# The norms' inverse roots as the exponential of minus half a logarithm on ScalarE, in a two-block transformer kernel

## The reference

```python
def rmsnorm(x, w):
    y = x32 * lax.rsqrt(jnp.mean(x32 * x32, axis=-1, keepdims=True) + EPS)
    return (y * w.astype(jnp.float32)).astype(x.dtype)

u = rmsnorm(h, norm1_w[l]) * (1.0 + sc1) + sh1            # block 1, before w_in
o = rmsnorm(o, gnorm_w) * jax.nn.silu(g...)               # HGRN2, per head
o = rmsnorm(o, subln_w) * (1.0 - lambda_init)             # differential attention, per head
u = rmsnorm(h, norm2_w[l]) * (1.0 + sc2) + sh2            # block 1, before the FFN
return rmsnorm(h, final_norm_w)                           # end of block 1, and norm of block 2
o_gla = _rmsnorm(o_gla, gla_norm_w)                       # GLA, per head
y = ((o - mu) * lax.rsqrt(var + EPS))                     # retention, per head
```

## Time and profile before

| | us |
|---|---|
| median of 3 runs | 1471.68 (1471.09 to 1471.78) |
| the profiled execution | 1472.01 |
| its span in the trace | 1470.2 |
| PE busy | 1341.5 (91%) |
| PEld busy | 1035.8 (70%) |
| DVE busy | 655.6 (45%) |
| ACT busy | 484.3 (33%) |
| POOL busy | 84.6 (6%) |
| TensorE's mean granted clock | 0.961 of full |

### The profile page before, as it was taken

How to read it: one execution, slowest core, us unless ns; L and a number is a source line. 1 busy time by engine, 2 the same in 40 slices (tenths; PEclk the granted TensorE clock), 3 DMA queues, 4 the chain that set the end, 5 groups by cost and what they waited for, 6 DMA issues and landing times. The chain is left out here.

```text
span 1470.2 us, 18836 instructions
## 1 busy us (share of the span) xinstructions
PE 1341.5 (91%) x8119; PEld 1035.8 (70%) x8119; DVE 655.6 (45%) x978; ACT 484.3 (33%) x711; POOL 84.6 (6%) x73
## 2 busy tenths in 40 slices
PE   4778587899999999799999997799999999999996
PEld 4777476899998889679999996455544444555442
DVE  3678766674555586485655655311111111111111
ACT  3544354544444644444554544110000000000001
POOL 2023200010000121020200000000000000000000
PEclk8989797999999999899999998899999999999999
DMA  7727342476545435254455556689999999999870
GB/s 265 273 89 258 141 172 87 136 242 222 173 155 176 137 123 163 93 172 141 123 175 181 175 189 255 261 367 384 390 364 391 390 390 390 382 397 382 365 322 30
DMA packets 102165, 349.87 MB, mean 238 GB/s; under 512 B 5856, under 2 KB 9216, under 8 KB 77504
## 3 DMA queue, kind: packets, MB, share of 16 engines
q1 hardware_dynamic: 100654, 345.56, 62.7%
q0 software_dynamic: 1168, 2.99, 0.8%
q10 hardware_dynamic: 258, 0.10, 0.0%
HBM read 347.57 MB, written 1.05 MB: 237 GB/s over the span
## 5 line engine op out<-in xcount | busy, mean ns | idle before, releaser
L504 PE MATMUL bank<-XH,WHL 128*128 128x256 f32 x2928 | 546.1, 287 | 24.8 <-issue 9.1
L504 PEld LDWEIGHTS bank<-XH,WHL 128*128 128x128 f32 x2928 | 467.3, 195 | 29.0 <-issue 20.4
L504 PE MATMUL bank<-XL,WHL 128*128 128x256 f32 x1464 | 418.1, 286 | 0.0
L1222 DVE TENSOR_TENSOR WHL<-weights,WHL 128x1024 fp32r<-128x1024 f32 x223 | 279.4, 1270 | 199.8 <-ACT WHL L843 199.4
L843 ACT ACTIVATE WHL<-weights 128x1024 fp32r<-128x1024 f32 x223 | 232.0, 1055 | 208.3 <-PE bank L504 208.1
L504 PEld LDWEIGHTS bank<-XL,WHL 128*128 128x128 f32 x1464 | 285.8, 195 | 0.2
L665 PE MATMUL bank<-arena 128*128 128x128 f32 x512 | 124.8, 404 | 3.2 <-DVE arena L1600 3.2
L665 PEld LDWEIGHTS bank<-arena 128*128 128x128 f32 x512 | 123.5, 336 | 3.3 <-DVE arena L1600 3.3
L504 PE MATMUL bank<-WHL,XH 128*128 128x512 f32 x320 | 105.8, 405 | 12.0 <-DVE WHL L1222 12.0
L1611 DVE COPY arena<-bank 128x512 f32<-128x512 f32 x16 | 11.1, 692 | 171.6 <-PE bank L665 171.6
L1889 DVE TENSOR_TENSOR chainm<-bank,chainm 128x512 f32<-128x512 f32 x16 | 11.1, 692 | 170.8 <-PE bank L789 170.8
(11 more groups left out here) (309 smaller groups left out, 1258.1 us busy)
## 6 DMA issues: line engine op xcount, KB each, us to landing
weights<-in_w_in SPq DMA_DIRECT2D x58, 1024.0 KB, 5.0
weights<-in_w_ada SPq DMA_DIRECT2D x24, 1024.0 KB, 5.3
weights<-in_expert_w_gate SPq DMA_DIRECT2D x24, 1024.0 KB, 6.6
weights<-in_expert_w_up SPq DMA_DIRECT2D x24, 1024.0 KB, 9.6
arena<-in_expert_w_up SPq DMA_DIRECT2D x24, 1024.0 KB, 10.9
arena<-in_expert_w_down SPq DMA_DIRECT2D x24, 1024.0 KB, 14.1
weights<-in_expert_w_down SPq DMA_DIRECT2D x24, 1024.0 KB, 13.8
arena<-in_expert_w_gate SPq DMA_DIRECT2D x24, 1024.0 KB, 7.5
```

The lines of the kernel that those rows point to most:

```text
L504: ins = e.matmul(o, l, r, start=first, skip_group_check=True, stop=g.part == g.parts - 1 and k == g.kc - 1 and n == 2)
L1222: e.tensor_tensor(lo, unit_weights(g, u), hi, ALU.subtract).then_inc(S.w_lo, 1)
```

## The change

Each `Sqrt` on ACT becomes `Ln`, and a second activation behind it, `Exp` with scale -0.5, writes the inverse root into the same tile; DVE's 20 reciprocals of these tiles go. The waits follow: DVE waits for the `Exp`, PE gets its bank back after the `Ln`, as it did after the `Sqrt`. The small activations that loaded the table of roots become `Ln` of a one. The tokens' norms of block 2 (L1171, L2154) keep their root and reciprocal.

```diff
             def norm_rms(i, after):
                 w.wait_ge(S.consts, 2)
-                e.activation(small[:, 40:41], epsc[:, 0:1], ACT.Sqrt).then_inc(S.sqrt_table, 1)
+                e.activation(small[:, 40:41], ones[:, 0:1], ACT.Ln).then_inc(S.sqrt_table, 1)
                 for k in range(KC):
                     squares(i, k, after(k))
                 w.wait_ge(S.ss, i + 1)
-                e.activation(rstd[:, :], bank[4][:, 0:T], ACT.Sqrt, bias=epsc[:, 0:1],
+                e.activation(rstd[:, :], bank[4][:, 0:T], ACT.Ln, bias=epsc[:, 0:1],
                              scale=1.0 / D).then_inc(S.rms, 1)
+                w.wait_ge(S.rms, i + 1)
+                e.activation(rstd[:, :], rstd[:, :], ACT.Exp, scale=-0.5).then_inc(S.rstd, 1)
...
                     w.wait_ge(*L.at(L.ss, h + 1))
-                    e.activation(L.rs[:, h, :], bank[4 + h % 2][:, 0:T], ACT.Sqrt, bias=epsc[:, 0:1],
+                    e.activation(L.rs[:, h, :], bank[4 + h % 2][:, 0:T], ACT.Ln, bias=epsc[:, 0:1],
                                  scale=1.0 / L.dv).then_inc(L.rms, 1)
+                    w.wait_ge(*L.at(L.rms, h + 1))
+                    e.activation(L.rs[:, h, :], L.rs[:, h, :], ACT.Exp, scale=-0.5).then_inc(L.rstd, 1)
                 yield
...
-                        e.activation(ak[:, h, :], bank[6][:, 0:T], ACT.Sqrt, bias=epsc[:, 0:1],
+                        e.activation(ak[:, h, :], bank[6][:, 0:T], ACT.Ln, bias=epsc[:, 0:1],
                                      scale=1.0 / P).then_inc(S.da_r, 1)
+                        w.wait_ge(S.da_r, 2 * h + 1)
+                        e.activation(ak[:, h, :], ak[:, h, :], ACT.Exp, scale=-0.5).then_inc(S.da_r, 1)
...
-            def norm_rstd(i):
-                w.wait_ge(S.rms, i + 1)
-                e.reciprocal(rstd[:, :], rstd[:, :]).then_inc(S.rstd, 1)
-
...
-                for h in range(HEADS):
-                    w.wait_ge(*L.at(L.rms, h + 1))
-                    e.reciprocal(L.rs[:, h, :], L.rs[:, h, :]).then_inc(L.rstd, 1)
                 yield
...
-                        w.wait_ge(S.da_r, h + 1)
-                        e.reciprocal(ak[:, h, :], ak[:, h, :]).then_inc(S.da_d, 1)
-                        w.wait_ge(S.da_d, 2 * h + 1)
+                        w.wait_ge(S.da_r, 2 * h + 2)
```

More of the change, by code:

```diff
@@ L200, in build @@
                                               "turned_copy", "values", "out", "squares", "sums", "rms", "done")]
-        diff_base = dict(zip([s.num for s in diff_sems], [8, 8, 20, 16, 8, 16, 4, 4, 4, 4, 4, 4, 4, 8]))
+        diff_base = dict(zip([s.num for s in diff_sems], [8, 8, 20, 16, 8, 16, 4, 4, 4, 4, 4, 4, 8, 4]))
         hst = Region(b1.at)
@@ L410, in build @@
         S.r1, S.rs2 = sem("first_norm_sum"), sem("second_norm_sum")
-        S.u2, S.fin_a, S.fin_v, S.fin = (sem("first_norm_" + n) for n in ("u", "rms", "rstd", "out"))
+        S.u2, S.fin_a, S.fin = (sem("first_norm_" + n) for n in ("u", "rstd", "out"))
         S.zz, S.z, S.dec_a, S.dec_v, S.gb = (sem("gla_" + n) for n in (
@@ L599, in diff @@
                         e.matmul(bank[6][:, 0:T], ones[:, :], aq[:, h, :], start=True, stop=True).then_inc(S.da_ss, 1)
-                        free[6] = (S.da_r, h + 1)
+                        free[6] = (S.da_r, 2 * h + 1)
                     yield
@@ L1037, in retention @@
                     w.wait_ge(*r.at(r.s2, i + 1))
-                    e.activation(mean[lane], bank[b0][:, 0:T], ACT.Sqrt, bias=epsc[:, 0:1],
+                    e.activation(mean[lane], bank[b0][:, 0:T], ACT.Ln, bias=epsc[:, 0:1],
                                  scale=1.0 / 512).then_inc(r.rms, 1)
+                    w.wait_ge(*r.at(r.rms, i + 1))
+                    e.activation(mean[lane], mean[lane], ACT.Exp, scale=-0.5).then_inc(r.rstd, 1)
                     yield
@@ L1043, in final_norm @@
                 w.wait_ge(S.rs2, 1)
-                e.activation(r1[:, :], r1[:, :], ACT.Sqrt, bias=epsc[:, 0:1], scale=1.0 / D).then_inc(S.fin_a, 1)
+                e.activation(r1[:, :], r1[:, :], ACT.Ln, bias=epsc[:, 0:1], scale=1.0 / D).then_inc(S.fin_a, 1)
+                w.wait_ge(S.fin_a, 1)
+                e.activation(r1[:, :], r1[:, :], ACT.Exp, scale=-0.5).then_inc(S.fin_a, 1)
                 yield
@@ L1096, in scalar @@
             for k in range(4, KC):
-                split_x(8 + k, k, mixT[:, k, :], (S.da_d, 2 * (k - 3)))
+                split_x(8 + k, k, mixT[:, k, :], (S.da_d, k - 3))
             run(gemm("wo1"))
@@ L1116, in scalar @@
             w.wait_ge(S.consts, 3)
-            e.activation(rstd[:, :], rstd[:, :], ACT.Sqrt, bias=eps2[:, 0:1], scale=1.0 / D).then_inc(S.rms, 1)
+            e.activation(rstd[:, :], rstd[:, :], ACT.Ln, bias=eps2[:, 0:1], scale=1.0 / D).then_inc(S.rms, 1)
+            w.wait_ge(S.rms, 3)
+            e.activation(rstd[:, :], rstd[:, :], ACT.Exp, scale=-0.5).then_inc(S.rstd, 1)
             for k in range(KC):
@@ L1524, in retention @@
                     yield
-                    w.wait_ge(*r.at(r.rms, i + 1))
-                    e.reciprocal(mean[lane], mean[lane]).then_inc(r.rstd, 1)
                     w.wait_ge(*r.at(r.rstd, i + 1))
@@ L1534, in final_norm @@
             def final_norm():
-                w.wait_ge(S.fin_a, 1)
-                e.reciprocal(r1[:, :], r1[:, :]).then_inc(S.fin_v, 1)
-                w.wait_ge(S.fin_v, 1)
+                w.wait_ge(S.fin_a, 2)
                 w.wait_ge(S.u2, KC)
@@ L1623, in vector @@
             weigh(0)
-            norm_rstd(0)
             for n in range(1, 4):
@@ L1682, in vector @@
             run(gemm("wo1", residual(16, 0)))
-            norm_rstd(1)
             norm_apply(1, 16, 8, 24)
@@ L1702, in vector @@
                                    op1=ALU.add).then_inc(S.rs2, 1)
-            norm_rstd(2)
             w.wait_ge(S.rstd, 3)
```

## The result

The changed kernel takes 1486.2 us, the median of 4 runs (1485.4 to 1487.1), beside 1471.7 us for the kernel before on the same chip (4 runs, 1471.1 to 1472.7): 1.0098 times as long, 95% interval 1.008 to 1.0115. It is slower, by 14.5 us. The profiled execution took 1485.91 (span 1484.1), 13.9 more than that of before.

What follows compares the result with a forecast made beforehand. PE, busy 91% of the span, bounds the kernel; the change counts where PE waits for a norm. Terms 0.5 + 8.6 + 6.5 - 0.7 + 0.2 = 15.1 us on 1472.0 give 1487.1, median 1486.8; range 1481 to 1493.5.

Steps and rivals of the forecast that it cites:

- The price of a load: Each of ACT's 29 added table loads takes 1.28 us, 1.30 until the next activation, with no drain on top.
- The rival at twice that: A load costs about 1.3 us more before each of a dozen dependent activations: 15 more, 1502 us; 4%.
- A single norm costs nothing: Ahead of the FFN, logarithm, load and exponential take 2.23 us for 2.26 before; zero for the joint norm too.
- HGRN2 and differential attention, 8.6: HGRN2 heads with the attention heads around them: `wo0` starts 8.0 us later, plus 0.6 for the fourth attention head.
- the fourth attention head: Before two weight splits for `wo1`: ACT arrives 1.72 us later, DVE is 1.75 lighter; 0 to 1.7, taken 0.6.
- My low of 7.4: The lowest cost in us given for HGRN2 and differential attention when all lows were summed; the high was 9.7.
- GLA, 6.5: GLA heads: pitch 3.22 to 4.97 us, three times 1.75, plus slower clock and restart; 5.25 to 7.6, taken 6.5.
- Start of block 2, -0.7: The load ahead of L1005 goes, 1.28 us less before ACT's splits, so PE's gap of 0.7 closes.
- Retention and final norm, 0.2: Exponentials and loads on ACT replace reciprocals ahead of DVE's splits, which start as before: 0.2 us, 5 if ACT's slack failed.
- The 12% rival: ACT becomes the bound in the retention: 1490 to 1492 us; 12%.
- First modulation, +0.5: Sums may start 0.8 us earlier, against shared DMA and a lower PE clock: -0.8 to +2.3, taken 0.5.
- The rival "a load costs nothing": Loads on the path are absent or hidden, so the exponential's 0.42 us replaces 1.75: 5 us faster, 1467; 3%.

Runs made afterwards that it cites:

- e7: Kernel before, roots and reciprocals kept, plus an unread 128x1 exponential behind each HGRN2 and GLA head's root, adding two table loads a head: 1483.6 us, ratio 1.0086.
- e4: Changed kernel, but the eight HGRN2 and GLA heads keep root and reciprocal as before: 1473.0 us, 1.0012 of the kernel before.
- e3: Kernel before, with logarithm and exponential on ScalarE only in the HGRN2 and GLA heads: 1484.2 us, ratio 1.0088.
- e1: Changed kernel with one table set for logarithm and exponential, loaded explicitly ahead of each norm or group of heads: 1470.1 us, 0.9996 of the kernel before.
- e5: As e1, but the first norm has root on ScalarE and reciprocal on VectorE as before: 1469.3 us, 0.9986 of the kernel before.
- e8: As e5, with the four squarings of each HGRN2 or GLA group ahead, one load behind the first: 1455.7 us, 0.9890 of the kernel before.
- e9: Kernel before, roots and reciprocals kept, with the four squarings of each HGRN2 or GLA group ahead of the first root: 1467.8 us, ratio 0.9978.
- e2: Changed kernel with each HGRN2 or GLA group's four exponentials behind its four logarithms, 12 loads fewer: 1476.8 us, 1.0035 of the kernel before.
- e10: Changed kernel with the four squarings of each HGRN2 or GLA group ahead, loads still at each logarithm and exponential: 1482.7 us, 1.0085 of the kernel before.
- e6: Kernel before, with only the first norm as logarithm and exponential on ScalarE, no reciprocal: 1473.5 us, ratio 1.0014.
- e11: As e6, with two unread 128x128 reciprocals on VectorE where the first norm's reciprocal stood: 1470.8 us, 1.0000 of the kernel before.

## Why the prediction was right

The time was 1486.8 forecast and 1486.2 measured. That they are only 0.6 apart is in part luck: the terms were 1.1 too high in sum, and I had set the median 0.3 below the profiled execution, where it came out 0.3 above. (My lower end stands as 1482 in one place and as 1481 in another; the time lies in either.) Step by step, as PE's instructions stand in the two traces:

- **The price of a load**, 1.30 with nothing behind it, held: 1283 ns, and the next activation 0.01 us later. The rival at twice that is out. The drain of 1380 ns that the Trainium skill has beside it ("ScalarE: Activation LUTs", "What ACT_TABLE_LOAD costs") stands in no row here: in e7 the load that starts at 225.68 ends at 226.96, and the next activation starts at 226.97.
- **A single norm costs nothing**: right, 2.23 for 2.26.
- **HGRN2 and differential attention, 8.6**: the pitch of 3.88 (forecast 3.9) and the 8.5 of `wo0` against before contain +0.7 from the start (the shift at 206.2, ahead of the first attention heads' roots). Up to `out_of_hgrn` the stage cost 243.15 - 234.62 - 0.7 = 7.8, for 8.0. The term that was too large is the fourth attention head: 0.6 taken, from 0 to 1.7, and the shift went from 8.5 at `wo0` to 8.2 at 264.0. So 7.5 in all, for 8.6. My low of 7.4 doesn't follow from my own terms, 8.0 and 0 to 1.7. That DVE's lighter load took it up there is argued, not shown.
- **GLA, 6.5**: 6.0 measured, in the lower half of 5.25 to 7.6. The pitch was 4.95 (4.97 forecast), in ACT's timeline of the changed kernel:

```profile
605.17 0.47 ACT L953 ACTIVATE arena<-bank,epsc 128x256 f32<-128x256 f32 x1 [0.86 <-PE bank L558]
...
620.01 0.47 ACT L953 ACTIVATE arena<-bank,epsc 128x256 f32<-128x256 f32 x1 [0.93 <-PE bank L558]
```

  and in that of before the first root, which answers to 605.17:

```profile
597.12 0.47 ACT L951 ACTIVATE arena<-bank,epsc 128x256 f32<-128x256 f32 x1 [0.86 <-PE bank L558]
```

  From the first to the last it is 14.84 for 605.84 - 597.12 = 8.72, so +6.1: three times 1.73 and the 0.9 by which the first pitch had been shorter before, at full clock, which I had as 0 to 0.95. That is the whole of the 6.0; of the 0 to 1.4 for a slower restart nothing came. How early the clock falls among these sums differs between executions by up to 1 us (e4 above), so that 6.0 is one draw; e3 had 6.5.
- **Start of block 2, -0.7**: -0.95 from 496.8 to 585.1, in every kernel without that load, and no gap at 505. Behind the joint norm's pause ahead of it the changed kernel lost 1.0 (from 480.2 to 496.8), as the clock rose later (0.67 from 492 to 496, against 0.96 at the matching 484 to 488 of before); I had zero. It isn't the norm's change that does it: e4, e1, e5 and e8 lost 0.6 to 1.0 there too, but so did e9 (1.0), whose joint norm is that of before, and e2 and e10 lost nothing with the changed one. e9's row at the matching place, with a clock of 0.68:

```profile
482.60:486.60 4.00, 4.00 (x26) 4.00 (x26) 2.16 (x4) 2.14 (x3) 3.28 (x6) 0.68 0.23 40
```

  What remained of both is -0.1.
- **Retention and final norm, 0.2**: -0.1. PE's gap is 1.93 for 2.05. The 12% rival, ACT as the bound there, did not come.
- **First modulation, +0.5** (-0.8 to +2.3): +0.7 at 206.2, by another road than I had described. `hf` started 0.5 earlier; then +2.4 stood at 87.5, as PE's clock fell behind an unchanged pause of 2.8 us, and a part of it was absorbed in later waits. I had the clock in the bound, as a fall next to w_ada only; that fall came as well, and took 1.6 (-2.1 at 42.7, -0.5 at 49). In e6, which holds this term alone, it is worth 1.9 us.

The terms measured are 0.7 + 7.5 - 0.1 + 6.0 - 0.1 = 14.0, for 15.1. The mechanism was right, and the sum some 1 us high.

**The rival "a load costs nothing"** is what e1 makes true by hand. Its price, 1467, was 3 us low. I had GLA at nothing and it cost 2.0; HGRN2 with its attention heads was to give 1.7, from items that I named but didn't add up, and gave nothing from 206.2 to 264.0 (the load ahead of the squaring took it); the first norm's loss (1.3 at 206.2) was not in it. Against that the retention's end gave 2.7 (665.2 to 985.7), which I did not have: with one set PE's gap of 2.05 us is gone. The Trainium skill's rule beside it ("ScalarE: Activation LUTs", "Table sets: the hidden batching unit": logarithm and then exponential take one load) describes what the hardware can do, and the runs agree once the kernel loads that set itself. The compiler's own placement did not do so for this kernel: 59 loads against 27.

## What to carry to other kernels

A function moved to ScalarE is priced with the table loads of the compiled order, and a load counts where the next thing in a serial chain stands behind it: here eight heads with two loads each lost 13 us, while the norm ahead of the FFN, where load and exponential took the reciprocal's time, lost nothing. Look for one set that serves both functions, and load it once, behind an instruction that needs no load of its own, where it hides (here the squaring, ahead of which the compiled order never has one). Leave out an explicit load whose set is already in place: it isn't dropped. Then look at the chain again: the set alone gave 2 us and the order alone 3, and both together 16, since each removed what hid the other.

## What the runs showed that I had not expected

- Behind the same PE pause of 2.8 us (73.1 to 75.9 before), the granted clock from 76 to 80 was 1.00 in six traces and 0.50 to 0.67 in seven, among them one of a kernel whose instructions up to there are those of before (e9). From 49 to 87 us the seven lost 1.9 to 3.1 us against before, the six lost nothing. The same stands behind the joint norm's pause (4.9 us, or 3.6 with one set): six of the traces lost 0.6 to 1.0 us, seven nothing, changed and unchanged norms among both. What decides it between executions stays open.
- A wait that nobody would count, PE's for a transfer that lands when it lands, cost 1.9 us by being longer: VectorE came free 1.75 us earlier, and PE got nothing from it but a lower clock. e11 gets the time back with two useless reciprocals.
- An activation on a 128x1 tile, with its neighbours on the same engine, took 0.20 us, so that a table switch can be added to a kernel and timed nearly by itself (e7).
